# One program of two networks on one core: the schedule around two attention layers is rewritten

## The reference

```python
def diff_mixer(h, w_in, lam, subln_g, w_out, cos, sin, lambda_init):   # first network, layer 2
    proj = jnp.einsum('btd,de->bte', h, w_in)
    q, k, v = jnp.split(proj, 3, axis=-1)
    q = apply_rope(q ...)                        # 8 heads, each with 2 halves of 64
    k = apply_rope(k ...)
    s = jnp.einsum('bqhcd,bshcd->bhcqs', qb, k) * scale
    p = masked_softmax(s, key_pos[None, :] <= tq[:, None])
    a = p[:, :, 0] - lam_val * p[:, :, 1]
    o = rms_norm(a @ v, subln_g) * (1.0 - lambda_init)
    return jnp.einsum('bte,ed->btd', o, w_out)

def moba_attention(h, w_qkv, w_o, rel_bias):     # second network, layer 2; one block of 256 keys
    q, k, v = jnp.split(h @ w_qkv, 3, axis=-1)   # 16 heads of 64
    p = softmax(q @ k.T * scale + bias[t5_bucket(distance)], causal)
    return (p @ v) @ w_o
```

## Time and profile before

| | us |
|---|---|
| median of three executions | 1328.47 |
| the profiled execution | 1326.24 |
| its span, first to last instruction | 1324.4 |
| PE busy | 1219.8 (92%) |
| VectorE busy | 847.3 (64%) |
| ScalarE busy | 574.4 (43%) |
| mean granted TensorE clock | 0.939 |
| DIFF, from PE's second half of chunk 0 to the start of its chunk 15 | 439.97 to 574.41 |
| MOBA, from PE's chunk 2 to the start of its chunk 15 | 1009.07 to 1120.67 |

### The profile page before, as it was taken

The page is one execution under the profiler, slowest core; times in us unless marked ns, Lnnn a source line. Parts: engine busy times, 40 slices in busy tenths (PEclk is TensorE's granted clock), DMA queues, the critical chain, the costliest instruction groups (busy, mean ns, idle before and its releaser), DMA issues.

```text
span 1324.4 us, 18386 instructions
## 1 busy us (share of the span) xinstructions
PE 1219.8 (92%) x7598; PEld 1071.9 (81%) x7598; DVE 847.3 (64%) x1276; ACT 574.4 (43%) x837; POOL 44.6 (3%) x86
## 2 busy tenths in 40 slices
PE   4989998999999988789999957999999899899997
PEld 3984776899998867579999847999988697899996
DVE  5662544587777766668777765977776445655554
ACT  5302231554444544455444455444446443744442
POOL 1010000000000000000000000000001100000000
PEclk9998556999999998899999978999999999899999
DMA  7933010488776423238877603977755432265530
GB/s 286 205 122 128 35 63 30 150 306 323 281 278 223 187 96 128 96 122 321 332 278 278 217 28 157 363 282 280 283 190 193 141 141 99 99 236 186 185 139 32
DMA packets 35746, 248.96 MB, mean 188 GB/s; under 512 B 4272, under 2 KB 4288, under 8 KB 6608
## 3 DMA queue, kind: packets, MB, share of 16 engines
q1 hardware_dynamic: 26352, 189.13, 38.3%
q0 software_dynamic: 9168, 57.56, 12.7%
q10 hardware_dynamic: 144, 1.11, 0.2%
HBM read 243.06 MB, written 4.19 MB: 187 GB/s over the span
## 4 chain that ended last, share of the span: by engine, by line
PE 81%; DVE 11%; ACT 4%; issue 2%; DMA 1%; DVEq 0%; SPq 0%; ACTq 0%
PE bank L1143 68%; DVE wlo L598 3%; PE bank L1318 2%; ACT whi L366 1%; PE bank L1502 1%; PE bank L1332 1%; DMA raw<-in_stream 1%; PE bank L1374 1%; DVE x L616 1%; DVE work L614 1%; PE bank L1221 1%; DVE ul L643 1%; PE bank L1385 1%; PE bank L1339 1%; PE bank L1341 1%
## 5 line engine op out<-in xcount | busy, mean ns | idle before, releaser
L598 DVE TENSOR_TENSOR wlo<-raw,whi 128x2048 fp32r<-128x2048 f32 x175 | 398.7, 2283 | 133.1 <-ACT whi L366 133.0
L1143 PE MATMUL bank<-uh,whi 128*128 128x256 f32 x1280 | 370.6, 289 | 2.9 <-DVE ul L643 2.9
L1143 PE MATMUL bank<-ul,whi 128*128 128x256 f32 x1280 | 363.6, 284 | 0.0
L1143 PE MATMUL bank<-uh,wlo 128*128 128x256 f32 x1280 | 363.5, 284 | 0.0
L366 ACT ACTIVATE whi<-raw 128x2048 fp32r<-128x2048 f32 x175 | 332.4, 1906 | 71.3 <-PE bank L1143 62.3
L1143 PEld LDWEIGHTS bank<-uh,whi 128*128 128x128 f32 x1280 | 246.9, 193 | 11.0 <-issue 8.9
L1143 PEld LDWEIGHTS bank<-ul,whi 128*128 128x128 f32 x1280 | 247.0, 193 | 4.7 <-issue 2.6
L1143 PEld LDWEIGHTS bank<-uh,wlo 128*128 128x128 f32 x1280 | 246.8, 193 | 0.0
L1143 PE MATMUL bank<-whi,hh 128*128 128x512 f32 x544 | 214.9, 395 | 0.0
L1143 PE MATMUL bank<-wlo,hh 128*128 128x512 f32 x544 | 212.9, 391 | 0.0
L1143 PE MATMUL bank<-whi,hl 128*128 128x512 f32 x544 | 212.2, 390 | 0.0
(11 more groups left out here) (229 smaller groups left out, 1157.8 us busy)
## 6 DMA issues: line engine op xcount, KB each, us to landing
raw<-in_stream SPq DMA_DIRECT2D x178, 1024.0 KB, 4.9
qk<-in_w_mod POOLq DMA_DIRECT2D x48, 1024.0 KB, 6.0
bias_rows<-PT POOLq DMA_DIRECT2D x1, 3072.0 KB, 36.3
u<-bias_rows POOLq DMA_DIRECT2D x16, 128.0 KB, 2.5
con<-in_con ACTq DMA_DIRECT2D x1, 1083.5 KB, 6.9
x<-in_x SPq DMA_DIRECT2D x2, 512.0 KB, 8.3
vo<-in_fin_g POOLq DMA_DIRECT2D x2, 512.0 KB, 4.3
out_y<-vo SPq DMA_DIRECT2D x2, 512.0 KB, 2.6
```

The lines of the kernel that those rows point to most:

```text
L598: nc.vector.tensor_tensor(wlo[:, c % RING, 0:w], raw[:, raw_index(c) % RING, 0:w], whi[:, c % RING, 0:w].bitcast(fp32), ALU.subtract).then ...
L1143: ins = mm(out, st, mv, start=start and i == 0, stop=stop and i == 2, skip_group_check=True)
```

## The change

- `MIXER`: the third pair of feature chunks (j = 2 and 6) goes ahead of the second pair of value chunks; banks are assigned anew.
- The second pair of value chunks is used one chunk at a time (`rows_of_values`), both tiles of tokens from one chunk and then both from the next. ACT copies the two value banks as each is done (`value_copy`).
- `hi_upto(chunk + 3)` moves to quarter 1, behind the other ACT work there (`hi_beside`). `lo_upto(chunk + 2)` stands at the end of quarter 3 from chunk 2 on (`lo_beside`).
- DIFF's rotation: DVE writes the sin product to `work` and the cos product back into the bank, PE adds the permuted product into the bank (`start=False`), and ACT copies the bank to `qk`. PE issues the permutation ahead of the other steps of the quarter.
- DIFF's transposed probabilities are copied by ACT, into two alternating buffers; in MOBA by DVE as before.
- Each phase has its own tables, and `combine` has one (`JOIN_AT`).

```diff
 MIXER = (("v", 0, 0), ("v", 0, 1), ("f", 0, 2), ("f", 4, 0), ("f", 1, 1), ("f", 5, 2),
-         ("v", 1, 0), ("v", 1, 1), ("f", 2, 2), ("f", 6, 0), ("f", 3, 1), ("f", 7, 2))
+         ("f", 2, 1), ("f", 6, 2), ("v", 1, 0), ("v", 1, 1), ("f", 3, 0), ("f", 7, 2))
-SCORE_AT = {(4, 3): 0, (5, 1): 1, (6, 3): 2, (7, 1): 3, (10, 3): 4, (11, 1): 5, (12, 3): 6, (13, 1): 7}
...
+SCORE_AT = {"d": {(4, 2): 0, (5, 2): 1, (6, 3): 2, (8, 0): 3, (9, 0): 4, (10, 0): 5, (12, 2): 6, (13, 0): 7},
+            "b": {(4, 1): 0, (4, 3): 1, (6, 1): 2, (6, 3): 3, (9, 0): 4, (10, 0): 5, (12, 1): 6, (12, 3): 7}}
+JOIN_AT = {(5, 1): 0, (6, 1): 1, (7, 2): 2, (8, 3): 3, (9, 3): 4, (10, 3): 5, (13, 1): 6, (13, 3): 7}
+TURN_AT = {"d": {(5, 2): (0, 0), (6, 2): (1, 0), (7, 3): (2, 0), (9, 0): (3, 0),
+                 (10, 0): (4, 0), (11, 0): (5, 0), (13, 2): (6, 0), (14, 0): (7, 0)},
+           "b": {(5, 1): (0, 0), (5, 2): (0, 1), (5, 3): (1, 0), (6, 0): (1, 1), (7, 1): (2, 0), (7, 2): (2, 1),
+                 (7, 3): (3, 0), (8, 0): (3, 1), (10, 1): (4, 0), (10, 2): (4, 1), (11, 1): (5, 0), (11, 2): (5, 1),
+                 (13, 1): (6, 0), (13, 2): (6, 1), (13, 3): (7, 0), (14, 0): (7, 1)}}
+VALUE_AT = {"d": {(5, 3): 0, (6, 3): 1, (8, 0): 2, (9, 1): 3, (10, 2): 4, (11, 1): 5, (13, 3): 6, (14, 1): 7},
+            "b": {(5, 3): 0, (6, 1): 1, (7, 3): 2, (8, 1): 3, (10, 3): 4, (11, 3): 5, (13, 3): 6, (14, 1): 7}}
+OUT_AT = {"d": {(7, 2): 0, (10, 0): 1, (12, 0): 2, (14, 3): 3},
+          "b": {(6, 3): 0, (8, 3): 1, (12, 1): 2, (14, 3): 3}}
...
+            def hi_beside(m0, i, q):
+                if 1 <= i < 15 and q == 1:
+                    hi_upto(m0 + i + 3)
...
+            def lo_beside(m0, i, q):
+                if i >= 2 and q == 3:
+                    lo_upto(m0 + i + 2)
...
+            def rope_in_place(b, q, r):
...
+                link(nc.vector.tensor_tensor(t2, src, sn, ALU.mult))
+                return nc.vector.tensor_tensor(src, src, cs, ALU.mult)
...
-                    rope_parts(bank[k], 2, j < 4, r).then_inc(d_t2, 1)
-                if feature and q == 2:
-                    dve.wait_ge(d_sw, r + 1)
-                    rope_sum(qk[:, 2 * j:2 * j + 2, :], bank[k], 2, r).then_inc(d_add, 1)
...
-                if q == 1:
-                    lo_upto(min(DIFF + i + 3, MLP1 + 1))
...
+                    rope_in_place(bank[k], j < 4, r).then_inc(d_t2, 1)
+                if (i, q) in JOIN_AT:
+                    combine(JOIN_AT[i, q])
+                if (i, q) in VALUE_AT["d"] and VALUE_AT["d"][i, q] % 2:
+                    sub_norm(VALUE_AT["d"][i, q] // 2)
+                if (i, q) in SCORE_AT["d"]:
+                    pair_maxima("d", SCORE_AT["d"][i, q])
+                if (i, q) in OUT_AT["d"]:
+                    pair_lower(1, OUT_AT["d"][i, q], lam[:, 6:7])
+                lo_beside(DIFF, i, q)
```

More of the change, by code:

```diff
@@ L496, in _, with value_copy @@
                     hi_upto(10 + (i - 6) // 4)
[L497 to L503, removed]
+            def value_copy(h, t, base, m, done):
+                if t == 0:
+                    act.wait_ge(v_ps, base + h + 1)
+                else:
+                    act.wait_ge(used, m + 1)
+                nc.scalar.activation(v_[:, t, 512 * h:512 * h + 512], bank[t][:, :], ACT.Copy).then_inc(done, 1)
+            def hi_beside(m0, i, q):
+                if 1 <= i < 15 and q == 1:
+                    hi_upto(m0 + i + 3)
             out_upper(0, one)
@@ L528, in _ @@
                     nc.scalar.activation(msq[:, 0, 0:4], msq[:, 0, 0:4], ACT.Sqrt, scale=1.0 / 128).then_inc(r_sd, 1)
-                if (i, q) in OUT_AT:
-                    pair_upper(1, OUT_AT[i, q], lam[:, 6:7])
+                if (i, q) in SCORE_AT["d"]:
+                    pair_exps("d", SCORE_AT["d"][i, q])
+                hi_beside(DIFF, i, q)
             for t in range(NT):
@@ L557, in _ @@
             for i, q in QUARTERS:
[L558 to L574, removed]
+                if (i, q) in ((1, 3), (9, 3)):
+                    value_copy(i // 8, 0, 2, MOBA + i, b_v)
+                elif (i, q) in ((2, 0), (10, 0)):
+                    value_copy(i // 8, 1, 2, MOBA + i - 1, b_v)
+                    if i == 2:
+                        spread_copy(3, cb, 6)
+                if q == 0 and 1 <= i <= 12 and MIXER[i - 1][0] == "f":
+                    _, j, k = MIXER[i - 1]
+                    act.wait_ge(used, MOBA + i)
+                    b = bank[k][:, :].rearrange("p (t n) -> p t n", t=2)
+                    nc.scalar.activation(qk[:, 2 * j:2 * j + 2, :], b, ACT.Copy, scale=HD ** -0.5 if j < 4 else 1.0)\
+                        .then_inc(b_copied, 1)
+                if (i, q) in OUT_AT["b"]:
+                    pair_upper(2, OUT_AT["b"][i, q], one)
+                if (i, q) in SCORE_AT["b"]:
+                    pair_exps("b", SCORE_AT["b"][i, q])
+                hi_beside(MOBA, i, q)
             act.wait_ge(mod_ready, 3)
@@ L735, in turned_copy @@
             def turned_copy(ph, p, c):
[L736 removed]
+                n = 2 * p + c
                 dve.wait_ge(s_tr[ph], n + 1)
@@ L1103, in _ @@
             for i, q in QUARTERS:
[L1104 to L1109, removed]
+                if (i, q) in TURN_AT["b"]:
+                    turned_copy("b", *TURN_AT["b"][i, q])
+                if (i, q) in VALUE_AT["b"] and VALUE_AT["b"][i, q] % 2:
+                    j = VALUE_AT["b"][i, q] // 2
                     dve.wait_ge(s_exp["b"], 4 * j + 4)
@@ L1118, in _ @@
                     ins.then_inc(o_sc, 1)
[L1119 to L1122, removed]
+                if (i, q) in SCORE_AT["b"]:
+                    pair_maxima("b", SCORE_AT["b"][i, q])
+                if (i, q) in OUT_AT["b"]:
+                    pair_lower(2, OUT_AT["b"][i, q], one)
+                lo_beside(MOBA, i, q)
             dve.wait_ge(spread_out, 8)
@@ L1573, in _, with rows_of_values, both_halves @@
                     ins.then_inc(oc_ps, 1)
-            def both_halves(m, e=None, steps=None):
+            def rows_of_values(m, g, steps):
+                pe.wait_ge(lo_ready, m + 1)
+                for t in range(NT):
+                    ins = half_values(m, g, t, None, lambda t, q: steps(2 * t + q % 2))
+                    if t == 0 and g == 1:
+                        ins.then_inc(v_ps, 1)
+                ins.then_inc(used, 1)
+            def both_halves(m, e):
                 for g in range(2):
@@ L1584, in both_halves @@
                             ins.then_inc(v_ps, 1)
-                        if e is not None and t == 0 and g == 0:
+                        if t == 0 and g == 0:
                             norm(e, 1)
```

109 lines of the change are left out of this document (58 added, 51 removed).

## The result

The changed kernel took 1308.28 us (median of four runs, 1304.68 to 1311.43) and the kernel before 1329.34 us beside it (four runs). The ratio is 0.985, 95% interval 0.981 to 0.988: 1.5% faster, and the forecast of 1309 held. A second comparison (e0) gave the same answer.

The account below looks back on a forecast made before the run. PE, busy 92%, was taken to bound the kernel, losing time waiting for `combine` and `turned_copy`. Gains 16.1 + 10.9 less 2.0, 2.6 and 1.0 make 21.4, less 2.0 for handovers 19.4: forecast 1309 us, range 1302 to 1321.

Parts of the forecast that it names:

- The account of the stretches: DIFF and MOBA to chunk 15: length less PE's full-clock work, 25.0 and 11.6 us lost; 16.1 and 10.9 gained.
- the walk: Three new engine queues followed quarter by quarter at profiled prices; gives PE 7.3 us of waits in DIFF, 0.7 in MOBA.
- handovers with little to spare: Nine handovers with under half a us to spare in the queues; 2.0 us taken off the gain for them.
- The waits: PE's remaining waits in DIFF, 7.3 us in all, the largest 3.9 in chunk 7, quarter 1, behind DVE's queue.
- The table load: ACT in DIFF's (6, 3): 1.28 us with nothing following; the skill's rule of 2.66 per switch would make the wait 5.3.
- The clock after it: Half clock behind the 3.9 us wait in DIFF's chunk 7, costing 1.4 to 1.9 us, taken as 1.6.
- The product into the bank: DVE's cos product in DIFF's rotation: between 0.61 us and twice that, near end taken, plus 0.1 for a link.
- The exits: Late MLP lower splits delay the first tile's residuals behind chunk 15's start: 2.0 us lost in DIFF, 2.6 in MOBA.
- The sum: Whole kernel: 16.1 + 10.9 - 2.0 - 2.6 - 1.0 = 21.4 us gained, including 1.0 for a clock fall at DIFF's exit.
- A: DIFF: DVE's queue is late more often, at (9, 1), (11, 1), (14, 1); 16.5 us less gain, 1325; chance 0.1.
- D: Mixers' chunk starts: PE waits for the lower split, 2.2 us per start, 53 in all, so slower, 1335; chance 0.04.
- B: Clock and exits eat more: remaining long waits and both MLP starts at half clock, about 3 + 3 us, 1315; chance 0.17.

Follow-up runs that it names:

- e0: The changed kernel run again with no edit, against the kernel before: 1307.14 us, ratio 0.986.
- e5: The kernel before with only its lower splits late, at the end of quarter 3 for chunk i+2: 1323.75 us, ratio 0.997.
- e10: The changed kernel with both upper and lower splits where the kernel before has them: 1307.52 us, ratio 0.985.
- e2: The changed kernel with the lower split of DIFF's chunk 8 behind the rotation of (7, 0): 1300.91 us, ratio 0.981.
- e7: The changed kernel with the second value chunks used as a pair again: 1309.04 us, ratio 0.986.
- e6: The changed kernel with the rotation as before, both products to work tiles and VectorE adding: 1307.93 us, ratio 0.986.
- e1: The changed kernel with lower splits back in quarter 1 for chunk i+3, upper ones left late: 1341.29 us, ratio 1.011.
- e8: e2 with both MLP chunks split ahead of the exit, lower splits in (14, 0) and (14, 2): 1299.32 us, ratio 0.979; again 1302.75 us, 0.980.
- e3: The changed kernel with the MLP's first lower split in (14, 2), the second behind the second tile's scaling: 1310.40 us, ratio 0.988.
- e9: e8 with the lower splits of DIFF's chunks 12 and 13 also behind the rotations of (11, 0) and (12, 0): 1300.61 us, ratio 0.980.
- e4: e3 with DIFF's lower split of chunk i+1 behind the rotation in quarter 0 of chunk i: 1310.23 us, ratio 0.987.

## Why the prediction was right, and where its reasons were not

*The account of the stretches* held. Measured against 16.1 and 10.9 us of gain by the walk stand 14.9 and 9.9. The 2.2 missing are as large as the 2.0 that I took off for handovers with little to spare, but they are not those handovers. In DIFF PE stood still for 7.4 us, 7.3 predicted, and the 1.2 missing is the clock (below). In MOBA it stood still for 1.4, 0.7 predicted.

*The waits.* Predicted 3.9 in (7, 1), 0.7 before chunk 10, 0.9 in (11, 1), 0.45 in (12, 1) and in (13, 3), 0.35 in (14, 3), 0.5 before chunk 15. The timeline has 3.93, 0.57, 0.94, 0.61 and, for the last three, under 0.2, 0.44 and 0.27; one of 0.32 at an earlier swap was not predicted. The chain of the changed kernel shows the one that mattered as the prediction walked it (start us, us, what):

```profile
488.63 0.60 ACT u L549
...
489.25 1.28 ACT L551
490.53 0.01 issue
490.54 0.21 ACT msq L551
...
492.85 2.20 DVE wlo L622
495.05 0.61 DVE work L802
...
495.69 0.71 DVE bank L803
496.40 0.04 issue
496.44 2.08 PE bank L1639 x2
```

*The table load* (489.25) is 1.28 us and the root starts 0.01 after it, with a second load for the exps ahead of their maxima. The drain of about 1.38 us per load that the Trainium skill (ScalarE: Activation LUTs, What ACT_TABLE_LOAD costs) counts does not show, and the wait is 3.93 and not 5.3: to go by the row was right.

*The clock after it* was mis-sized: 2.76 us of DIFF were lost to half clock, 1.6 predicted. I took the fall behind one of the waits of the earlier trace rows; this one lasted from 495.1 to 501.9, 5.5 us of it behind the wait, which ended at 496.44. At DIFF's exit no fall came where I had taken 1.0.

*The product into the bank*, the one unseen price, is L803 below (groups of VectorE by shape, count | busy us, mean ns | idle before). 699 ns beside 686 for the same product to `work`: the near end of the bounds was right.

```profile
L803 DVE TENSOR_TENSOR bank<-bank,con 128x512 f32<-128x512 f32 x8 | 5.6, 699 | 0.3
L802 DVE TENSOR_TENSOR work<-bank,con 128x512 f32<-128x512 f32 x8 | 5.5, 686 | 7.3 <-PE bank L1174 7.3
```

*The exits*: 2.0 and 2.6 predicted, 1.76 and 2.68 measured. A longer stretch of half clock behind MOBA's exit cost 1.4 in the last MLP, which the sum lacks; e0 does not have it.

*The sum*: 21.4 less 2.0, so 19.4; measured 19.3 without the stretch ahead of DIFF, and the medians differ by 21.1 and 19.6 (e0). That the profiled sum agrees to 0.1 is luck: the fall in DIFF was priced 1.2 too low and MOBA's gain 1.0 too high, half clock in the last MLP (1.4) was not foreseen, the fall at DIFF's exit (1.0) did not come, and the 2.0 for handovers covered the balance. Rivals A and D are refused by the waits above: inside both stretches none is over 2 us at another place, and none is for a split at a chunk's start. The one other wait over 2 us is the 4.21 at MOBA's exit, which the prediction had priced as the exit's loss. B is refused by the table: beyond the one fall in DIFF the clock took 1.4 us in this execution and nothing in e0, where B had 3 + 3. D's price was also added up wrongly: 1309 has the 27 gained already in it, so 53 more make about 1360 and not 1335. Nothing else hangs on that number.

*What was not right is the share of the parts.* The text put the early lower split first among the reasons why PE waits, and the walk never asked what each part brings alone. The chain ahead of the longest wait in the kernel before (7.84 us) has the early lower split in it, and ahead of it what the prediction names second, an upper split that could start only when PE had left a chunk, with the maxima behind the split of a finished group (`hh`):

```profile
490.96 1.60 PE bank L1143 x6
...
492.64 1.91 ACT whi L366
494.55 0.58 ACT hh L448
...
497.02 2.20 DVE wlo L598
...
499.86 0.49 DVE P L1007
...
500.39 0.69 PE bank L1385 x2
```

Three kernels beside the kernel before show the shares (gains in us against it, by the table's method; the clock in unchanged code is left out):

| | DIFF | MOBA | exits | sum |
|---|---|---|---|---|
| old order, lower splits late, upper ones early (e5) | 6.9 | 3.0 | -4.4 | 5.5 |
| all the rest of the change, both splits early (e10) | 13.6 | 7.0 | 0.0 | 20.6 |
| all of it, both splits late (the change) | 14.9 | 9.9 | -4.4 | 20.4 |

Both cure the same late `combine`: PE waits 17.2 us for it in DIFF before, 8.5 in e5, 4.0 in e10 and not at all in the changed kernel. So their gains do not add. In the new order the late splits bring 1.3 + 2.9 and cost 4.4 at the exits: nothing in sum. They paid once the collision in (7, 1) was mended: e2 stands at 0.981 with the long exits still in it. What e10 would gain from such repairs was not tried, nor was the new order with the lower splits alone late.

What e10 keeps of the change is several parts. e7 gives the single value chunks 2.2 us beside late splits, e6 gives the rotation next to nothing. The order of the feature chunks, the tables and ScalarE's copies of the transposed probabilities were not tried apart, so which of them carries the rest is open. One thing in the tables changed for every pair of heads: from a pair's score step to its first turn there were three quarters before, and there are four in DIFF and four or five in MOBA now. That is at least 1.4 us more cover for each turn; no run shows what it is worth alone.

## What to carry to other kernels

- Measure the gain by stretch, as the lost time (length less full-clock work), and count what each part brings alone: two edits that cure the same wait each look like the cause.
- When work is split between two engines, do not put the second half ahead of where the first half is made: everything behind it in its in-order queue waits too, 32.7 us in DIFF (e1), against 4.0 with both halves early (e10). Moving the second half alone to a later place did no such harm (e5).
- Work put at the end of a loop's quarters lands on the exit, where the next stage needs the same engine. Do its last pieces ahead of the exit (e8: exits 4.4 us shorter), not behind it, where PE waits for them (e3: nothing gained).

## What the chip showed beside that

- TensorE's clock does not answer to a wait alone. Behind 1.79 us of idle it went to 0.5 in e9, behind 1.80 us at the same place of e8's second execution, and 1.79 of its first, it stayed at 1.00 (fences above for two of the three). In DIFF the wait of 3.93 brought a fall, and that of 1.74 in e2 none. The fall in e9 cost 1.7 us, that in DIFF of the changed kernel 2.8.
- It also falls where PE's record shows no idle time in the ten us around it, in code that no kernel here changes. In the 10 us from 35, first the changed kernel, then the kernel before:

```profile
35.00:45.00 10.00, 10.00 (x68) 9.52 (x67) 4.28 (x5) 2.02 (x2) 0.00 (x0) 0.81 0.99 119
```
```profile
35.00:45.00 10.00, 10.00 (x79) 9.04 (x78) 5.08 (x7) 3.85 (x3) 0.00 (x0) 1.00 0.99 124
```

  Six of the fourteen profiled executions have a fall there (the changed kernel's, e1, e4, e6 and both of e8). With it DIFF's stretch of the changed kernel starts at 443.75, without it, in e0, at 439.81. Those 3.9 us are over half of the 6.7 between the fastest and the slowest of its first four runs. What makes it fall there is open.
